# Norms, rotation and gates of two mixers placed beside the input projections, and another block order in the local attention

## The chip, the cores and the metric

The kernel runs on one core of one Trainium2 chip. The metric is the device time of one execution in microseconds (us), lower is better. The core has five engines with queues of their own: TensorE (PE in the rows; its weight loads PEld), VectorE (DVE), ScalarE (ACT), GpSimd (POOL) and SyncE (SP), which here issues the DMAs. They meet only at semaphores.

## The reference, cut to what matters

A block of four layers runs over 512 latent tokens and 256 context tokens of width 1024, all in float32. Layer 1 ("even") joins local attention with a gated linear recurrence; layer 2 is a retention layer; layers 3 and 4 join a convolution, a differential attention and a delta-rule recurrence. The change touches layer 1 and layers 3 and 4. Of layer 1:

```python
k_ctx = kv_heads(pc['a_k'], qk_g[1])                 # RMS norm per head of 64
q_lat = apply_rope(attn_q_heads(p['a_q'], qk_g[0]), cos, sin)
k_lat = apply_rope(kv_heads(p['a_k'], qk_g[1]), cos, sin)
a_lat = window_attention(q_lat, k_lat, kv_heads(p['a_v']), k_ctx, v_ctx, sink)
f = lb + (1.0 - lb) * sigmoid(f_raw)                 # gates of the recurrence
q_l = silu(b_q);  y = rms_norm(o) * silu(b_g)
def apply_rope(x, cos, sin):
    x1, x2 = xf[..., :half], xf[..., half:]
    return concatenate([x1 * cos - x2 * sin, x2 * cos + x1 * sin])
```

A block of 128 queries sees the 256 context keys and, if it lies in the latent part, the key blocks beside it. Blocks 0 and 1 are the context's own queries, so they see 2 key blocks; blocks 2 to 5 see 4, 5, 5 and 4. Of layers 3 and 4 the change touches how 24 rows of the projection become the gates of the delta rule: beta = sigmoid(b) and g = -exp(A_log) * softplus(a + dt_bias), summed along each chunk of 128 tokens, and exponentials of these sums.

## The kernel before, in words

Activations lie transposed: 128 channels down the partitions, the 768 tokens (context, then latent) along a row. A tile `core.u(t)` is such a strip. A projection (`Dense`, L267) makes output in groups of 256 columns: for each of 8 input tiles k, 2 halves f and each token segment it does three float32r matmuls of split high and low halves (L476 to L478). Two sets of banks alternate between groups, so group g+2 waits for group g to be evacuated. ScalarE evacuates a group, then makes the high half of the weights of group g+2 (L259), and VectorE the low half (L264). A `side` object hangs other work on this loop: `side.scalar` and `side.vector` are called after each group on these engines, `side.tensor` on TensorE after input tile 3 of a group, and `side.load` on SP between weight loads. In layer 1's projection (13 groups, 0 to 12) the side work is `Modulation` (L953): VectorE multiplies and adds conditioning weights (L1013, L1016), and TensorE sums them over partitions with one-column matmuls (L1035) in groups 1, 3, 5, 7 and 9.

Stages are blocks of instructions; at the end of each, all engines meet. After layer 1's projection come:

- `head_norm` "qk" (L1484): squares on ScalarE, sums per head by matmuls of 10 rows (L1535), root, reciprocal on VectorE (L1554), spread back by matmuls (L1546), multiply (L1561), for the five tiles of queries and keys.
- `rope_stage` (L1573): six tables by DMA; the rotated half by a matmul with a permutation (L1591); values transposed (L1593); multiply and add on VectorE and GpSimd; keys copied to both head halves by matmuls (L1598, L1599). Beside it ScalarE applies sigmoid and silu to 16 tiles (L1622 to L1624).
- `window_stage` (L1634): 24 steps, for each of 4 pairs of heads the blocks 0 to 5. TensorE makes scores of step s+2, turns the probabilities of step s in chunks (L1722) and weighs the values of step s-1 (L1735). ScalarE does the exponentials (L1769) and copies the turned chunks (L1778); VectorE takes the maximum (L1796), normalises (L1813) and takes the outputs away (L1820).
- `gla_stage` (L1832), the recurrence, and its norm.

In layers 3 and 4 the projection of 13 groups has `Convolutions` (L2510) as side work. Then `delta_gates_stage` (L2744) makes the gates and turns keys and values (24 transposes, L2766), and `mixer_stage` (L2828) runs delta rule and attention in one interleaved order. It opens with value transposes (L3088), while SP loads a table `dist` and four lambda vectors (L2903, L2905) that GpSimd waits for before it casts the table (L3269) and makes the first slope (L3220); the first attention scores (L3045, L3052) need both.

## Time and profile before

| | |
|---|---|
| time, median of 3 runs | 4082.05 us (4080.58 to 4082.73) |
| the profiled execution's own time | 4088.78 us |
| span of its trace | 4087.0 us |
| mean granted TensorE clock | 0.947 of full |
| PE busy | 3805.1 us (93%) |
| DVE busy | 2240.8 us (55%) |
| ACT busy | 1530.3 us (37%) |
| POOL busy | 341.6 us (8%) |

Shares of busy time are means over some forty stages. What a stage costs is read from where it starts and ends, and what binds it from the waits inside it.

### The profile page before, as it was taken

Reading aid. Unit: us, or ns where it says so; the run is one execution under the profiler, and the core shown is the slowest. Engines: PE = TensorE matmul, PEld = TensorE weight load, DVE = VectorE, ACT = ScalarE, POOL = GpSimd, SP = SyncE. Lnnn points to the kernel's source line nnn. Section 1 sums busy time; section 2 is a strip of 40 time slices with the busy share of each in tenths; the row PEclk is TensorE's granted clock in tenths of the full one; section 3 lists DMA queues with packets and bytes.
Section 4 is the critical chain, followed back from the end, with each engine's and each line's share of the span. In section 5 each row is a group of like instructions: output and inputs, shape, how many; then the busy total and the mean of one; then the engine's idle time right before and its main releaser. Section 6 shows DMA issues by size and latency. Waiting matters only on the chain. (4 is left out here: it accounts for less than half of the span.)

```text
span 4087.0 us, 49821 instructions
## 1 busy us (share of the span) xinstructions
PE 3805.1 (93%) x20537; PEld 3114.3 (76%) x20537; DVE 2240.8 (55%) x3209; ACT 1530.3 (37%) x2348; POOL 341.6 (8%) x292
## 2 busy tenths in 40 slices
PE   7998789999999999999999979989998979988998
PEld 4884567888887888878877758757787757867886
DVE  5724765545465444572266756544477856544375
ACT  2114632111354322352254335433365335533264
POOL 0000220000000000000000045200000034400000
PEclk9997879999999999999999979979999979988999
DMA  5510012333212121123222100022222200012231
GB/s 199 176 42 10 6 42 81 126 124 129 69 61 75 64 66 60 62 76 100 92 96 91 58 12 1 1 83 78 94 96 83 68 12 1 1 63 76 88 103 62
DMA packets 254721, 288.91 MB, mean 71 GB/s; under 512 B 6756, under 2 KB 226939, under 8 KB 254517
## 3 DMA queue, kind: packets, MB, share of 16 engines
q1 hardware_dynamic: 252437, 281.84, 21.4%
q10 hardware_dynamic: 2080, 4.19, 0.3%
q8 instruction: 146, 2.39, 0.2%
q14 instruction: 58, 0.48, 0.0%
HBM read 283.92 MB, written 2.10 MB: 70 GB/s over the span
## 5 line engine op out<-in xcount | busy, mean ns | idle before, releaser
L476 PE MATMUL banks<-h_halves,w_halves 128*128 128x512 f32 (+1 forms) x3728 | 1391.9, 373 | 56.3 <-DVE h_halves L264 32.4
L477 PE MATMUL banks<-h_halves,w_halves 128*128 128x512 f32 (+1 forms) x3728 | 1387.2, 372 | 0.0
L478 PE MATMUL banks<-h_halves,w_halves 128*128 128x512 f32 (+1 forms) x3728 | 1380.4, 370 | 0.0
L476 PEld LDWEIGHTS banks<-h_halves,w_halves 128*128 128x128 f32 x3728 | 713.5, 191 | 196.4 <-issue 49.4
L478 PEld LDWEIGHTS banks<-h_halves,w_halves 128*128 128x128 f32 x3728 | 711.5, 191 | 122.3
L477 PEld LDWEIGHTS banks<-h_halves,w_halves 128*128 128x128 f32 x3728 | 713.5, 191 | 117.6 <-issue 0.5
L264 DVE TENSOR_TENSOR w_halves<-work,w_halves 128x2048 fp32r<-128x2048 f32 (+1 forms) x212 | 481.3, 2270 | 434.8 <-ACT w_halves L259 434.5
L259 ACT ACTIVATE w_halves<-work 128x2048 fp32r<-128x2048 f32 (+1 forms) x212 | 401.4, 1894 | 409.0 <-PE banks L478 388.6
L259 ACT ACTIVATE h_halves<-kept 128x512 fp32r<-128x512 f32 (+1 forms) x520 | 332.1, 666 | 301.4 <-PE banks L478 231.5
L264 DVE TENSOR_TENSOR h_halves<-kept,h_halves 128x512 fp32r<-128x512 f32 (+1 forms) x520 | 360.8, 736 | 133.0 <-ACT h_halves L259 132.3
L1016 DVE SCALAR_TENSOR_TENSOR kept<-kept 128x512 f32<-128x512 f32 x280 | 188.2, 744 | 7.2 <-DMA kept<-in_mod_w 7.2
L758 ACT ACTIVATE kept<-kept 128x512 f32<-128x512 f32 x64 | 37.5, 631 | 234.3 <-DVE kept L752 234.2
L2211 PE MATMUL banks<-h_halves,w_halves 128*128 128x512 f32 x320 | 120.5, 377 | 3.7 <-DVE h_halves L1181 3.7
L1207 POOL TENSOR_TENSOR h_halves<-kept,h_halves 128x768 fp32r<-128x768 f32 (+1 forms) x8 | 13.6, 1706 | 1304.4 <-ACT kept L1174 1304.4
L773 ACT ACTIVATE kept<-banks 128x512 f32<-128x512 f32 x66 | 30.0, 530 | 245.3 <-PE banks L478 245.3
L2212 PE MATMUL banks<-h_halves,w_halves 128*128 128x512 f32 x320 | 118.9, 372 | 0.0
L2213 PE MATMUL banks<-h_halves,w_halves 128*128 128x512 f32 x320 | 118.5, 370 | 0.0
L752 DVE SCALAR_TENSOR_TENSOR kept<-banks,kept 128x512 f32<-128x512 f32 x64 | 41.0, 685 | 139.4 <-PE banks L478 139.4
L3265 POOL TENSOR_TENSOR work<-work 128x512 f32<-128x512 f32 x84 | 108.8, 1300 | 70.5 <-PE banks L2938 52.6
L3397 DVE TENSOR_TENSOR work<-work,banks 128x512 f32<-128x512 f32 x84 | 62.5, 744 | 94.3 <-PE banks L2958 94.3
L2227 PE MATMUL banks<-w_halves,h_halves 128*128 128x256 f32 x384 | 108.7, 283 | 0.0
L2226 PE MATMUL banks<-w_halves,h_halves 128*128 128x256 f32 x384 | 108.7, 283 | 0.0
(388 smaller groups left out, 4973.7 us busy)
## 6 DMA issues: line engine op xcount, KB each, us to landing
work<-in_w_ff SPq DMA_DIRECT2D x64, 1024.0 KB, 5.3
work<-in_ffn_w_in SPq DMA_DIRECT2D x44, 1024.0 KB, 5.1
kept<-in_mod_w SPq DMA_DIRECT2D x40, 1024.0 KB, 5.1
work<-in_odd_w_in SPq DMA_DIRECT2D x24, 1024.0 KB, 5.4
work<-in_w_in SPq DMA_DIRECT2D x24, 1024.0 KB, 5.0
work<-in_ffn_w_out SPq DMA_DIRECT2D x16, 1024.0 KB, 5.2
work<-in_even_w_in SPq DMA_DIRECT2D x13, 1024.0 KB, 5.1
work<-in_odd_w_out SPq DMA_DIRECT2D x8, 1024.0 KB, 5.1
```

Source lines behind the costliest of these rows:

```text
L259: return core.nc.scalar.activation(dst, src, ACT.Copy)
L264: return core.nc.vector.tensor_tensor(dst, src, high.bitcast(F32), ALU.subtract)
L476: nc.tensor.matmul(o, low[:, k - a, fc], rh[:, tc], start=(k == 0), stop=False)
L477: nc.tensor.matmul(o, high[:, k - a, fc], rl[:, tc], start=False, stop=False)
L478: mm = nc.tensor.matmul(o, high[:, k - a, fc], rh[:, tc], start=False, stop=(k == K - 1))
L1016: ins = nc.vector.scalar_tensor_tensor(out=self.sum(q, n), in0=self.slot(m)[:, k], scalar=c, in1=self.sum(q, n), op0=ALU.mult, op1=ALU.add)
L2211: nc.tensor.matmul(o, low[:, c, fc], rh, start=(c == 0), stop=False)
L2212: nc.tensor.matmul(o, high[:, c, fc], rl, start=False, stop=False)
L2213: mm = nc.tensor.matmul(o, high[:, c, fc], rh, start=False, stop=(c == KD - 1))
L2226: nc.tensor.matmul(o, core.h(c)[:, tc], low[:, c, :], start=False, stop=False)
L2227: mm = nc.tensor.matmul(o, core.h(c)[:, tc], high[:, c, :], start=False, stop=(c == KD - 1))
L3265: nc.gpsimd.tensor_tensor(c4(pl.level[m % 3]), c4(pl.s[h % 2]), mat(pl.pairs[:, cc(lv)]), ALU.mult).then_inc(level_masked, 1)
```

## The change

Layer 1: `head_norm` "qk" and `rope_stage` are gone. A new side object `QueriesKeys`, which holds the old `Modulation`, does their work inside the projection: squares, head sums in groups 1 to 3, root and reciprocal after group 3, spreads in groups 6 to 8, norm and rotation on GpSimd, with the rotated half fetched by DMA from partition to partition and its sign put into the sine table; values turned in group 9. Sigmoid and silu are applied as ScalarE evacuates a group (`EvenCopy`), which now takes both segments; the context segments of the two halves share one bank. The local attention starts at once and takes the blocks in another order.

Layers 3 and 4: the gate arithmetic moves into `Convolutions` (groups 8 to 12). `delta_gates_stage` becomes `turn_stage`: 24 transposes, their copies split between VectorE and ScalarE, and the loads and cast that opened `mixer_stage`.

```diff
@@ class Dense
+                if side is not None:
+                    side.load_last(sp, low_done, units)
...
                             if side is not None and k == 3:
                                 side.tensor(pe, i * B + j)
+                            if side is not None and k == 6:
+                                side.tensor_late(pe, i * B + j)
+class EvenCopy(Finish):
+        def scalar(act, g, j, f, banks, half, free, done):
+            func = self.FUNC.get(g, ACT.Copy)
+            nc.scalar.activation(core.u(2 * g + f)[:, LAT], banks[0], func).then_inc(free, 1)
+            if f == 1:
+                o = core.sb(U0 + 2 * g * T, 2 * T).rearrange("p (f t) -> p f t", t=T)[:, :, 0:CTX]
+                nc.scalar.activation(o, core.ps[:, 4 + j % 2, :].rearrange("p (f t) -> p f t", t=CTX), func).then_inc(free, 2)
+class QueriesKeys:
+    SQUARES = {1: (0, 1), 2: (2, 3), 3: (4,)}
+    SPREADS, SPREADS_LATE = {6: 0, 7: 2, 8: 4}, {6: 1, 7: 3}
+    COPIES = {6: (0, 1), 7: (2, 3), 8: (4,)}
+    def load(self, sp, at):
+        self.mod.load(sp, at)
...
+        if at == 9:
+            sp.wait_ge(self.scaled, self.N)
+            sp.dma_start(self.cos, core.const("cosA")).then_inc(self.tables_in, 16)
+            sp.dma_start(self.sin, core.const("sinA")).then_inc(self.tables_in, 16)
+            self.swap(sp, 0)
+            self.swap(sp, 1)
+        if at == 10:
+            for m in range(2, self.N):
+                sp.wait_ge(self.roped, m - 1)
+                self.swap(sp, m)
+            sp.wait_ge(self.roped, self.N)
...
+    def scalar(self, act, at):
...
+        if at == 4:
+            act.wait_ge(self.square_used, self.N)
...
+        for m in self.COPIES.get(at, ()):
+            act.wait_ge(self.spread, m + 1)
+            if m:
+                act.wait_ge(self.scaled, m)
...
+        if at == 12:
+            act.wait_ge(self.roped, self.N)
+    def vector(self, dve, at):
+        if at == 4:
+            dve.wait_ge(self.rooted, 2)
+            self.nc.vector.reciprocal(self.std, self.std).then_inc(self.rstd_done, 1)
+        self.mod.vector(dve, at)
+    def gpsimd(self, pool):
+        for m, x in enumerate(self.tiles):
+            pool.wait_ge(self.copied, 2 * m + 2)
+            nc.gpsimd.tensor_tensor(x, x, self.back, ALU.mult).then_inc(self.scaled, 1)
+        pool.wait_ge(self.tables_in, 32)
+        for m, x in enumerate(self.tiles):
+            pool.wait_ge(self.swapped[m % 2], 64 * (m // 2 + 1))
+            nc.gpsimd.tensor_tensor(x[:, LAT], x[:, LAT], self.cos, ALU.mult).then_inc(self.turned, 1)
+            nc.gpsimd.tensor_tensor(o, o, self.sin, ALU.mult).then_inc(self.turned, 1)
+            pool.wait_ge(self.turned, 2 * m + 2)
+            nc.gpsimd.tensor_tensor(x[:, LAT], x[:, LAT], o, ALU.add).then_inc(self.roped, 1)
@@ window_stage
-    steps = [(p, i) for p in range(4) for i in range(6)]
+    steps = [(p, i) for p in range(4) for i in (2, 0, 3, 4, 1, 5)]
...
-            pe.wait_ge(masks_ready, 2)
@@ class Convolutions, tensor
+        if j == 10:
+            pe.wait_ge(self.centred, 2)
+            pe.wait_ge(self.gate_dve, 5)
+            for d in range(2):
+                nc.tensor.matmul(core.ps[:, 4, d * 24:(d + 1) * 24].rearrange("p (c n) -> p c n", n=6), pl.cum[d],
...
+        if j == 11:
+            pe.wait_ge(self.gate_act, 5)
@@ second_layer
-    delta_gates_stage(core, nc, a, l, pl)
+    turn_stage(core, nc, a, l, pl)
@@ mixer_stage
-            sp.dma_start(pl.dist, core.const("dist")).then_inc(loads_in, 16)
...
-            pe.wait_ge(dist_made, 1)
```

How the change moves instructions is shown at three places. First TensorE inside group 7 of layer 1's projection, after input tile 3; L1035 (L1040 in the changed kernel) are the one-column sums. Before:

```order
L476 MATMUL banks<-h_halves,w_halves 128x256
L477 MATMUL banks<-h_halves,w_halves 128x256
L478 MATMUL banks<-h_halves,w_halves 128x256
L1035 MATMUL banks<-kept 128x1 x16
L476 MATMUL banks<-h_halves,w_halves 128x512
```

and of the changed kernel (L1180 and L1181 are the spreads of a tile's inverse norm):

```order
L476 MATMUL banks<-h_halves,w_halves 128x256
L1040 MATMUL banks<-kept 128x1 x16
L1180 MATMUL banks<-kept 128x512
L1181 MATMUL banks<-kept 128x256
L472 MATMUL banks<-h_halves,w_halves 128x512
```

Two matmuls have been put behind the sums; ten such pairs are spread over groups 1 to 8.

Second ScalarE between the evacuation of group 5 and that of group 7. Before (L657 evacuates, L259 makes the high half of weights):

```order
L657 ACTIVATE kept<-banks 128x512 x2
L259 ACTIVATE w_halves<-work 128x2048
L657 ACTIVATE kept<-banks 128x512 x2
L259 ACTIVATE w_halves<-work 128x2048
L657 ACTIVATE kept<-banks 128x512 x2
```

In the changed kernel (L728 and L731 evacuate, L250 makes the high half, L1150 copies a spread out of its banks):

```order
L728 ACTIVATE kept<-banks 128x512 x2
L731 ACTIVATE kept<-banks 128x2x256
L250 ACTIVATE w_halves<-work 128x2048
L1150 ACTIVATE kept<-banks,kept 128x512
L1150 ACTIVATE kept<-banks,kept 128x256
L1150 ACTIVATE kept<-banks,kept 128x512
L1150 ACTIVATE kept<-banks,kept 128x256
L728 ACTIVATE kept<-banks 128x512 x2
```

The copies stand between a weight split and the next evacuation.

Third TensorE from the end of the third layer's projection into its mixer; the branches are stage ends. Before:

```order
L2761 MATMUL banks<-kept 128x24 x4
L2766 MATMUL banks<-kept 128x128 x24
L2772 MATMUL banks<-work 128x24 x2
L2774 MATMUL banks<-work,kept 128x48
L2749 UNCONDITIONAL_BRANCH
L2907 UNCONDITIONAL_BRANCH
L3088 MATMUL banks<-kept 128x128 x12
L2923 MATMUL banks<-kept,work 128x128 x4
L3045 MATMUL banks<-work 128x512 x2
L3052 MATMUL banks<-p_halves 128x512 x6
```

Of the changed kernel:

```order
L2944 UNCONDITIONAL_BRANCH
L2948 MATMUL banks<-kept 128x128 x24
L2936 UNCONDITIONAL_BRANCH
L3043 UNCONDITIONAL_BRANCH
L3224 MATMUL banks<-kept 128x128 x12
L3059 MATMUL banks<-kept,stream 128x128 x4
L3181 MATMUL banks<-work 128x512 x2
L3188 MATMUL banks<-p_halves 128x512 x6
```

The gate matmuls (L2761, L2772, L2774) have left the stage; they now stand in groups 8 and 10 of the projection.

## Rows read from the trace of the kernel before

**Rows 1.** Busy time by stretch, layer 1 after its projection; columns start:end, length, engines.
```profile
core 0: us, PE busy (x) PEld busy (x) DVE busy (x) ACT busy (x) POOL busy (x), PEclk, DMA share, GB/s
313.80:344.40 30.60, 24.84 (x48) 9.76 (x48) 11.53 (x15) 5.94 (x9) 0.00 (x0) 0.72 0.00 1
344.40:366.70 22.30, 12.29 (x24) 5.35 (x24) 8.07 (x10) 15.70 (x11) 6.32 (x5) 0.70 0.13 41
366.70:464.50 97.80, 85.70 (x721) 59.87 (x722) 67.06 (x192) 62.34 (x186) 0.74 (x2) 0.95 0.01 1
```
**Rows 2.** Timeline at stage ends; columns start, duration, instruction, idle before and releaser.
```profile
313.79 1.08 ACT L657 ACTIVATE kept<-banks 128x512 f32<-128x512 f32 x2 [15.71 <-PE banks L478]
315.16 3.83 ACT L1522 ACTIVATE work<-kept 128x768 f32<-128x768 f32 x5 [0.28 <-PEq L431]
366.89 1.28 ACT L1767 ACT_TABLE_LOAD   x1 [0.26 <-PEq L1579]
```
**Rows 3.** Busy time by stretch, groups 2, 3, 5 and 9 of layer 1's projection.
```profile
110.30:127.10 16.80, 16.80 (x97) 14.70 (x96) 13.70 (x21) 2.89 (x4) 0.00 (x0) 1.00 0.61 191
127.10:149.00 21.90, 21.90 (x129) 19.55 (x128) 13.19 (x20) 2.87 (x4) 0.00 (x0) 0.92 0.43 144
165.80:189.30 23.50, 23.50 (x129) 20.93 (x128) 13.20 (x20) 2.88 (x4) 0.00 (x0) 0.85 0.46 150
244.80:263.40 18.60, 18.60 (x113) 16.49 (x113) 3.05 (x4) 2.89 (x4) 0.00 (x0) 1.00 0.18 57
```
**Rows 4.** Timeline, TensorE, spreads in group 10 of the third layer's projection.
```profile
2322.37 2.84 PE L2698 MATMUL banks<-kept 12*128 12x512 f32 x6
```
**Rows 5.** Timeline, VectorE: side work in group 5, and the reciprocals of stage "qk".
```profile
176.29 0.88 DVE L1013 TENSOR_SCALAR kept<-kept 128x512 f32<-128x512 f32 x2 [5.30 <-PE banks L1035]
177.09 9.36 DVE L1016 SCALAR_TENSOR_TENSOR kept<-kept 128x512 f32<-128x512 f32 x14
...
325.12 4.95 DVE L1554 RECIPROCAL work<-work 10x512 f32<-10x512 f32 x2 [10.44 <-ACT work L1525]
```
**Rows 6.** Busy time by stretch, local attention, six steps of one pair of heads.
```profile
402.30:424.50 22.20, 20.48 (x183) 14.42 (x181) 16.76 (x50) 15.18 (x46) 0.00 (x0) 1.00 0.01 1
```
**Rows 7.** Timeline, local attention: its first matmul, and VectorE's longest wait in that stretch.
```profile
367.70 0.55 PE L1699 MATMUL banks<-work,kept 64*128 64x256 f32 x1 [2.74 <-POOL work L1758]
...
413.82 0.29 DVE L1820 COPY kept<-banks 128x128 f32<-128x128 f32 x1 [1.41 <-ACT work L1778]
```
**Rows 8.** Timeline, the third layer's gate stage: first instruction, transposes, sums.
```profile
2360.61 1.28 ACT L2814 ACT_TABLE_LOAD   x1 [9.55 <-PEq L431]
...
2360.97 4.50 PE L2766 MATMUL banks<-kept 128*128 128x128 f32 x24
2370.09 1.05 PE L2772 MATMUL banks<-work 128*128 128x24 f32 x4 [4.61 <-DVE work L2795]
2370.96 0.64 PE L2774 MATMUL banks<-work,kept 128*128 128x48 f32 x2
```
**Rows 9.** Timeline, opening of the third layer's mixer.
```profile
2374.86 2.80 PE L3088 MATMUL banks<-kept 128*128 128x128 f32 x12 [3.26 <-PEq L2749]
...
2376.68 0.43 SPq L2905 DMA_DIRECT2D work<-in_diff_lambda_k  x1
...
2379.50 1.28 DVE L3312 SCALAR_TENSOR_TENSOR p_halves<-kept,p_halves 128x512 fp32r<-128x512 f32 x2
...
2381.76 1.21 POOL L3269 CAST work<-kept 128x896 f16<-128x896 f32 x1 [551.28 <-DMA work<-in_diff_lambda_k]
...
2384.04 1.01 PE L3045 MATMUL banks<-work 128*128 128x512 f16 x2 [5.53 <-POOL work L3220]
2384.98 1.65 PE L3052 MATMUL banks<-p_halves 32*128 32x512 f32 x6
```
**Rows 10.** Busy time by stretch, groups 8 and 11 of the third layer's projection.
```profile
2293.50:2304.40 10.90, 10.90 (x49) 9.01 (x49) 10.27 (x15) 3.89 (x4) 0.00 (x0) 1.00 0.30 96
2331.00:2348.10 17.10, 17.10 (x59) 11.79 (x58) 10.45 (x9) 3.84 (x3) 0.00 (x0) 0.90 0.00 1
```

More of the change, by code:

```diff
@@ L537, in _ @@
                     group(G // B, j)
-            if before is not None:
-                block.gpsimd(before.gpsimd)
+            @block.gpsimd
+            def _(pool):
+                if before is not None:
+                    before.gpsimd(pool)
+                if side is not None:
+                    side.gpsimd(pool)
             def wait_tile(eng, i, n):
@@ L2516 @@
     SEMS = 22
+    LOADS = 16 * 5
     PAD = CONV_K // 2
@@ L2806, in _ @@
-            chain.wait()
-            nc.vector.tensor_tensor(pl.ekd, core.ps[:, 7, 48:96], pl.gsum, ALU.subtract).then_inc(sums, 1)
-            dve.wait_ge(chain_a, 2)
-            nc.vector.scalar_tensor_tensor(out=pl.nbge, in0=pl.beta, scalar=-1.0, in1=pl.eg, op0=ALU.mult, op1=ALU.mult)
+            for b in range(0, 6, 2):
+                dve.wait_ge(turned, b + 1)
+                nc.vector.tensor_copy(dst(b), bank(b))
         @block.scalar
         def _(act):
-            act.wait_ge(turned, 1)
@@ L2822, in _ @@
[L2822 to L2825 removed]
+            for b in range(1, 6, 2):
+                act.wait_ge(turned, b + 1)
+                nc.scalar.activation(dst(b), bank(b), ACT.Copy)
+        @block.gpsimd
+        def _(pool):
+            pool.wait_ge(loads_in, 16 * 6)
+            nc.gpsimd.tensor_copy(pl.dist16, pl.dist)
@@ L3498, in second_layer @@
     cat = (0, 1, 4, 5, 6, 19, 20, 21)
-    into.run(f"in2_{l}", before=before, side=Convolutions(core, nc, l))
     pl = DeltaPlan(core)
-    delta_gates_stage(core, nc, a, l, pl)
+    into.run(f"in2_{l}", before=before, side=Convolutions(core, nc, l, a, pl))
+    turn_stage(core, nc, a, l, pl)
     mixer_stage(core, nc, a, l, pl)
```

440 lines of the change are left out of this document (244 added, 196 removed).

## The prediction, made before the changed kernel was run

> **What bounds the kernel now.** I read the page first: TensorE is busy 93% of the span, so what counts is where it is not doing projection matmuls. The timeline gave the stage ends, the table of stretches each stage's length, and the timeline inside a stage who waits for whom. Between layer 1's projection and its local attention lie two stages of 30.6 and 22.3 us [rows 1] in which no engine is full: in "qk" TensorE is busy 24.8 us, VectorE 11.5; in the rotation ScalarE 15.7 of 22.3, TensorE 12.3. The granted clock there is 0.72 and 0.70, a mixture of 1.2 and 2.4 GHz. These are chains, each link waiting for the one before. The projection is the opposite: a group without side work lasts 16.80 us at clock 1.00 with TensorE busy all of it, while ScalarE works 2.89 us of it and VectorE 13.7 [rows 3]. So work on the slack engines is free there and each matmul costs its full length. The same holds for layers 3 and 4: a gate stage that is a chain of tiny instructions, from 2360.61 us [rows 8] to the mixer's start at 2374.86 [rows 9], behind a projection whose groups take 10.90 us [rows 10].
>
> The sum is made against the profiled execution, 4088.78 us, which is 6.7 us (0.16%) above the median of the runs, 4082.05; I take the difference over to the median.
>
> **The two stages removed.** From the first instruction of "qk" at 315.16 to the first of the local attention at 366.89 are 51.7 us [rows 2]. What takes their place at the projection's end: the last evacuation, two activations in 1.08 us [rows 2], becomes three of about 512 elements on ScalarE, +0.5. VectorE's copies beside it fall away but ran in parallel. Gain 51.2.
>
> **What layer 1's projection takes on.** TensorE gets 5 head sums and 5 spreads, each of a 512- and a 256-column float32 matmul. Three such matmuls of 512 columns took 2.84 us at the full clock [rows 4], 0.95 each; half that for 256; 1.42 a pair, 14.2 for ten. The six value transposes: 24 took 4.50 [rows 8], so 1.1. Nothing covers them: TensorE is full there. To this comes the clock. Groups with 8, 16, 16 one-column sums last 18.60, 21.90 and 23.50 [rows 3]. Eight cost 1.8 (18.60 - 16.80), so sixteen should cost 3.6, but cost 5.1 and 6.7, and exactly these two groups show a clock of 0.92 and 0.85: side work of this kind is followed by a stretch at 1.2 GHz, worth 1.5 or 3.1 us. The new pairs are longer matmuls; three of them left the clock at 1.00 as far as [rows 4] go, since they took no more than 0.95 each. I add 1.7 us for one more such stretch, most likely in group 7, where a pair stands right behind sixteen sums. The bounds are 0 and nine places times 3.1, 28. Total +17.0.
>
> The page of the Trainium skill on this, "TensorE: Matmul & The Clock Gate", section "What's actually happening", has the clock follow how busy TensorE has been. [Rows 3] do not agree as it stands: TensorE shows busy for 23.50 of 23.50 us in the group whose clock is 0.85. By the rule the new pairs would cost no clock and the sum below would be 1.7 us better; I go by the row.
>
> The other engines there cost nothing, and this is their cover. ScalarE: per group 0.5 for the context, squares of 0.8 each, copies of about 1 us, table loads of 1.28 [rows 2], at most 6 us more on 2.9 in a group of 16.8. Its copies in groups 6 to 8 wait for spreads after input tiles 3 and 6; behind them in its queue stands the next evacuation, which is due only at the group's end, one input tile (2.1 us) after the later spread, and TensorE needs its banks a whole group later. VectorE: the reciprocals, 4.95 us [rows 5], come after group 3 ahead of 10.2 us of conditioning work [rows 5]. VectorE then finishes some 4 us into group 5, and the sums in the middle of group 5 that wait for it are due 8.4 us in: hidden, with 4 us to spare. It loses its own evacuations, 0.75 a group. GpSimd does 5 multiplies and 15 rotation operations, 1.2 to 1.7 us each as in the stages before; with DMA hops of 3 to 5 us between tiles the rotation takes 25 to 35 us from the middle of group 8 and is due only before group 12's evacuation, some 60 us later. SP's queue: the load of unit 12 stands behind the wait for the norms in group 8 and is due two groups later. No cost; if any cover were gone, it would be a few us once.
>
> **The local attention.** Its first matmul waited for GpSimd's casts until 367.70 [rows 7], 0.8 us after the stage began; these casts are now earlier. It also begins right after full-clock matmuls instead of at 1.2 GHz, worth another 0.7 in its first steps. The block order: six steps take 22.20 us, TensorE busy 20.48, VectorE 16.76, ScalarE 15.18 [rows 6]. The waits are latencies of the loop maximum, exponentials, normalise, turn, copy; the longest of VectorE's four in this stretch is 1.41 us [rows 7]. Light blocks between heavy ones fill some of them, but the same five-block steps 3 and 4 still stand side by side, and the stage now starts with a heavier block. Following the queues with these durations I find each pair of heads about 0.5 us shorter, and as much lost again at the two ends. Bounds: better by 4 x (22.20 - 16.76) = 21.8, if only VectorE bound it; worse by two waits of 1.41 more per pair, 11.3. I take 0. Together -1.5.
>
> **The gate stages, twice.** Before, 14.25 us (2360.61 to 2374.86) [rows 8, 9]. After: the transposes, 4.9 us with the first copies behind them, run beside six DMAs. The last lambda vector is issued 1.8 us into the stage and landed 5.1 after its issue (2376.68 to 2381.76 [rows 9]), that is at 6.9; the larger table behind it in the same queue may add 1; then the cast, 1.21 [rows 9], and the stage end, 0.3: 9.4. Gain 4.9. What is late there is now GpSimd's load, no longer the chain.
>
> Then the mixer's opening. TensorE waited until 2384.04 for GpSimd's slope, itself behind the cast [rows 9]: the three-pass scores L3052 start at 10.12 us into the stage. With loads and cast gone the next to be late is VectorE's split, 2379.50 + 1.28 [rows 9], 5.92 us in. So they start at 6.0, 4.1 earlier, and the chain behind them moves along: GpSimd's own opening work, 5 us, no longer binds. Per layer 9.0, twice 18.0. Bounds per layer: 4.1 alone if the loads land as late as the old stage ended, and 11 if they land after 4 us.
>
> **What the second projection takes on.** Four small transposes and three small matmuls, ten instructions; six of them took 1.05 + 0.64 [rows 8], the rest about 0.9: 2.6 per layer, full price, in groups 8 and 10. The side work of group 11 made it 17.10 us where 10.90 is the rule, at clock 0.90 [rows 10], so a low-clock stretch of 1.5 more can follow in group 10; I keep that for the range. TensorE's new wait in group 11 for ScalarE's exponentials comes 5.4 us into the group by the queue's durations, where TensorE arrives at 5.45: a tie. Behind it are group 11's sums and spreads. Twice 2.6 is +5.2.
>
> **Sum:** -51.2 + 17.0 - 1.5 - 18.0 + 5.2 = -48.5. From 4082.05: 4033.5 us (profiled: about 4040).
>
> **Rivals.**
> 1. The clock. Each of the nine new places in layer 1's projection is followed by a low-clock stretch like group 5's. For it: [rows 3], three groups of one-column sums out of five show it. Against: [rows 4] do not. Price 28 - 1.7, so 4060.
> 2. The order pays. The waits of [rows 7] vanish halfway between TensorE's limit, 4 x (22.20 - 20.48) = 6.9, and VectorE's 21.8: 14 better, 4019.5. Against: the chain through one step is unchanged.
> 3. Slower than before. ScalarE waits before group 12's evacuation for the end of the rotation (a chain SP, DMA, GpSimd, SP through five tiles). From the middle of group 8 it has some 60 us until it delays anything, and must lose 48 more before the gain is gone: it would have to take 108 us, over 20 a tile, where its three operations and one hop come to 7. Then 4085 and more, us for us. Nothing in the rows supports it but that no such hop was measured.
> 4. The loads do not gain in the gate stages: DMAs of broadcast vectors, now with a table behind them, land later and the stages shorten by 2 instead of 4.9. Then 4039.
>
> **Chances:** forecast with its small deviations 0.66, clock 0.10, order 0.10, loads 0.12, slower 0.02. The predicted time is 4033.5. The range 4020 to 4048 holds the forecast, the loads, half of the order's case and the milder half of the clock's. A measurement of this kernel tells 0.2%, about 8 us, from no change; only rival 3 comes near, so faster 0.97, same 0.01, slower 0.02.
>
> **What would show it.** In the changed profile: layer 1's groups 1 to 3 and 6 to 9 longer by 1.4 to 3 us each and none by more than 4.5; the attention's first matmul within 2.5 us of the projection's last; no wait of TensorE on GpSimd's rotation; the attention 94 to 98 us; turn stages of 9 to 10 us ended by GpSimd's cast; the mixer's first scores about 6 us in. The forecast is wrong if the projection's clock falls below 0.9 over its length, or if a stage after it changes in length, which I take to be none.

## The result, and the profile after

The changed kernel takes 4047.55 us, median of 3 runs (4046.64 to 4048.96), against 4082.05: ratio 0.9917, 95% interval 0.9894 to 0.9939, 34.5 us faster. Run again on another chip it took 4042.13 (ratio 0.9896, 0.9881 to 0.9912). The forecast was 4033.5. The direction was right, and 14 of the 48.5 us are missing. From trace to trace the kernel lost 39.8 us (spans 4087.0 and 4047.2), 8.7 less than forecast. The other 5.3 come from the base: the profiled execution of before lay 6.7 us above its median, that of the changed kernel 1.4 above its own.

The profiled execution took 4048.96 us, its span is 4047.2. The time between the first instructions of the stages shows where the gain lies. "Again" is the second trace of the same kernel. Brackets in the column of before give the range over all four traces with that code (before, e2, e3, e4).

| us | before | after | after again | forecast of the difference |
|---|---|---|---|---|
| start of the local attention | 366.9 | 331.3 | 331.2 | -34.2 |
| local attention | 97.5 | 100.6 | 100.9 | -1.5 |
| recurrence | 102.9 | 105.6 | 105.4 | 0 |
| eight stages, to the third layer's projection | 1625.7 | 1625.8 | 1625.7 | 0 |
| projection and gate or turn stage, layer 3 | 181.9 | 180.5 | 180.0 | -2.3 |
| mixer, layer 3 | 296.8 (292.6 to 296.8) | 294.1 | 290.0 | -4.1 |
| projection and gate or turn stage, layer 4 | 196.0 | 194.0 | 192.3 | -2.3 |
| mixer, layer 4 | 296.7 (293.3 to 296.7) | 292.8 | 288.9 | -4.1 |

The busy time by stretch of the changed kernel answers to [rows 3]: groups 3, 5, 6, 7 and 8 of layer 1's projection, then group 12, the attention's first 3.9 us, the attention, and the recurrence.

```profile
core 0: us, PE busy (x) PEld busy (x) DVE busy (x) ACT busy (x) POOL busy (x), PEclk, DMA share, GB/s
132.10:155.60 23.50, 23.50 (x133) 19.88 (x132) 12.45 (x17) 5.38 (x6) 0.00 (x0) 0.93 0.39 123
172.40:194.30 21.90, 21.90 (x129) 19.53 (x128) 16.24 (x23) 4.66 (x5) 0.00 (x0) 0.92 0.60 195
194.30:214.50 20.20, 20.20 (x105) 16.16 (x105) 12.36 (x17) 5.50 (x9) 7.68 (x2) 1.00 0.60 205
214.50:241.20 26.70, 26.70 (x137) 21.72 (x136) 12.45 (x17) 5.46 (x8) 7.46 (x3) 0.87 0.13 41
241.20:259.70 18.50, 18.50 (x102) 15.46 (x101) 2.29 (x1) 4.43 (x6) 3.25 (x3) 1.00 0.35 107
...
312.60:329.40 16.80, 16.72 (x96) 14.47 (x94) 0.00 (x0) 1.53 (x3) 0.00 (x0) 1.00 0.00 0
...
331.10:335.00 3.90, 3.71 (x14) 2.40 (x14) 0.78 (x1) 1.28 (x1) 0.00 (x0) 0.56 0.00 0
...
331.10:431.90 100.80, 86.23 (x721) 60.70 (x721) 67.71 (x192) 61.73 (x186) 0.00 (x0) 0.94 0.00 1
431.90:537.50 105.60, 86.33 (x920) 76.86 (x920) 86.02 (x142) 51.43 (x67) 39.85 (x24) 0.76 0.02 6
```

The groups bear out the working: group 3 takes one pair on (21.90 to 23.50), group 6 two (16.8 to 20.2) at full clock, group 7 two beside its sums, with more low clock than before (21.9 to 26.8 at 0.87), group 8 one (16.8 to 18.5). Group 5, which takes nothing on, lost 1.6 us of low clock (23.50 to 21.90), but where such stretches fall varies: e2 has before's projection, and its groups 3, 5 and 7 last 23.5, 21.9 and 23.5 us for before's 21.9, 23.5 and 21.9. The attention's row is the one to stop at: 100.80 us with the same 721 matmuls that took 97.80 [rows 1]. The recurrence behind it has the same 920 matmuls too and is 2.7 us longer than before:

```profile
464.50:567.40 102.90, 83.50 (x920) 74.31 (x920) 85.62 (x142) 51.39 (x67) 39.87 (x24) 0.78 0.02 7
```

The timeline of the changed kernel, at the attention's start and at its end. Columns as in [rows 2].

```profile
331.26 1.28 ACT L1881 ACT_TABLE_LOAD   x1 [0.27 <-PEq L424]
335.87 0.20 ACT L1881 ACTIVATE kept<-kept 128x2 f32<-128x2 f32 x1 [3.33 <-DVE kept L1916]
335.99 0.67 ACT L1883 ACTIVATE work<-banks,kept 128x512 f32<-128x512 f32 x1
...
428.82 0.29 DVE L1934 COPY kept<-banks 128x128 f32<-128x128 f32 x1 [2.36 <-ACT work L1892]
429.26 1.97 PE L1855 MATMUL banks<-work,kept 128*64 128x128 f32 x16 [0.64 <-DVE kept L1934]
431.27 0.29 DVE L1934 COPY kept<-banks 128x128 f32<-128x128 f32 x1 [2.16 <-PE banks L1855]
431.84 1.28 ACT L1992 ACT_TABLE_LOAD   x1 [2.81 <-PEq L1806]
431.88 5.36 PE L2173 MATMUL banks<-kept 128*128 128x128 f32 x24 [0.65 <-PEq L1806]
```

The first exponential comes 4.7 us into the stage (335.99 against 331.26). Before it came 3.1 in, since block 0 has two key blocks and block 2 four (with the old order in the changed kernel it comes 2.5 in, e1, or 2.0, e12):

```profile
366.89 1.28 ACT L1767 ACT_TABLE_LOAD   x1 [0.26 <-PEq L1579]
...
369.96 0.46 ACT L1769 ACTIVATE work<-banks,kept 128x256 f32<-128x256 f32 x1
```

At the other end the last lines tell more. The last 16 weighing matmuls take 1.97 us, and the recurrence's first 24 transposes take 5.36 us, where the same instruction took 2.81 before. The rows show a granted clock of 0.50 there, TensorE's lower level. The stretches of the changed kernel's last steps:

```profile
424.00:428.00 4.00, 2.34 (x19) 1.64 (x18) 1.41 (x5) 0.88 (x2) 0.00 (x0) 0.88 0.00 0
428.00:432.00 4.00, 2.71 (x20) 1.97 (x20) 0.58 (x2) 0.97 (x3) 0.00 (x0) 0.50 0.00 0
432.00:436.00 4.00, 4.00 (x20) 4.00 (x21) 3.17 (x5) 1.13 (x1) 0.00 (x0) 0.50 0.48 131
```

Layer 3 after its projection, answering to [rows 8, 9]:

```profile
2333.74 2.81 PE L2948 MATMUL banks<-kept 128*128 128x128 f32 x24 [1.65 <-PEq L424]
...
2336.11 0.43 SPq L2942 DMA_DIRECT2D work<-tables  x1
...
2336.59 0.60 ACT L2962 ACTIVATE work<-banks 128x512 f32<-128x512 f32 x1 [0.27 <-PE banks L2948]
2342.55 0.93 POOL L2967 CAST work<-kept 128x896 f16<-128x896 f32 x1 [541.78 <-DMA work<-tables]
2343.81 2.79 PE L3224 MATMUL banks<-kept 128*128 128x128 f32 x12 [7.26 <-PEq L2936]
...
2349.97 1.65 PE L3188 MATMUL banks<-p_halves 32*128 32x512 f32 x6 [0.35 <-DVE p_halves L3445]
```

The turn stage lasts 10.1 us, and all its work is done by 2337.2, 3.5 us in. What ends it is GpSimd's cast, which waits for the sixth load, issued at 2336.11, until 2342.55. The mixer's three-pass scores start 6.16 us into it, as forecast (6.0), released by VectorE's split.

### The profile page after: what moved, and what is told of

It reads as the page before. It is cut to its first block and busy times, and to the rows that moved or that the text cites. A ratio compares the mean times of both kernels' runs of the same rounds, so it can differ in the third digit from the quotient of the medians.

```text
span 4047.2 us, 49776 instructions
## 1 busy us (share of the span) xinstructions
PE 3786.3 (94%) x20511; PEld 3106.7 (77%) x20511; DVE 2215.3 (55%) x3156; ACT 1541.4 (38%) x2377; POOL 375.5 (9%) x307
## 5 line engine op out<-in xcount | busy, mean ns | idle before, releaser
L250 ACT ACTIVATE w_halves<-work 128x2048 fp32r<-128x2048 f32 (+1 forms) x212 | 401.5, 1894 | 403.2 <-PE banks L476 382.9
L250 ACT ACTIVATE h_halves<-kept 128x512 fp32r<-128x512 f32 (+1 forms) x520 | 332.0, 665 | 302.0 <-PE banks L476 232.6
```

The source lines that it names most:

```text
L250: return core.nc.scalar.activation(dst, src, ACT.Copy)
```

## The experiments

Times are medians. Each ratio is to runs of before on the same chip; the experiments ran on four chips, where before took 4080.1 to 4084.0. The old order in the changed kernel comes first, since the attention's row asks for it.

**e1, the block order undone in the changed kernel; e12, the same again.**

```diff
-    steps = [(p, i) for p in range(4) for i in (2, 0, 3, 4, 1, 5)]
+    steps = [(p, i) for p in range(4) for i in (0, 1, 2, 3, 4, 5)]
```

> The changed kernel with the blocks of the local attention back in the order 0 to 5, all else kept. In the changed kernel this stage lasts 100.6 us where it lasted 97.5, against 96 forecast, and the recurrence behind it 105.6 where it lasted 102.9 with no edit. Theory A (the order costs): its first step now has a heavy block (first output 1.6 us later in the stage), each pair of heads takes 22.45 instead of 22.20, and the tail 0.5 more. Then this kernel's attention stage is 97 to 98 us, and the kernel is 2.5 to 3.5 us faster than the changed one, 38 faster than before (4044). Theory B (the order is neutral; the stage is longer because of where it starts, right behind full-clock matmuls, and what clock it is granted): the stage stays at 100 to 101 and the time at 4047 to 4048. On the recurrence: if its 2.7 us come from the order they go too (another -2.7, 4041); if they are the luck of where a low-clock stretch falls, they stay or move without a pattern.

Measured: 4035.40 us (4028.74 to 4046.43), ratio 0.9885 (0.9867 to 0.9903). Attention 97.0, recurrence 102.4. The stage is as theory A says, and the recurrence shortens too. The median is 12.2 us below the changed kernel's, but the two intervals overlap (the changed kernel's is 0.9894 to 0.9939), so what the order costs is read from the stages, over more traces.

**e11, the changed kernel again, beside e12.**

> The changed kernel once more, on the same chip as the next one, to measure what the block order is worth in pairs: from the traces 7.0 us (attention 3.55, recurrence 3.2), from the medians of two calls 12. Its time 4047 to 4048. If the recurrence shows 105.6 again with transposes of 5.4 us, that cost belongs to the order; if it shows 102.4 or 99.8, it is luck.

> The changed kernel with the blocks in the order 0 to 5, a second time, beside the run above. Its time was 4035.4 over a wide range (4028.7 to 4046.4). If the order costs 7 us by stages and the rest is scatter, this gives 4038 to 4041; if 12 is real, 4035. Its recurrence is 99.8 or 102.4, never 105.6, if the 2.8 us at the stage's boundary are the order's.

Measured: e11 4042.13 (ratio 0.9896, 0.9881 to 0.9912), e12 4034.60 (0.9885, 0.9871 to 0.9899). By stages: attention 100.9 against 95.9, recurrence 105.4 against 102.4. Over seven traces with the old order behind the new projection (e1, e12, e6, e15, e7, e10, e13) the attention takes 95.5 to 97.0, mean 96.4, and the recurrence 99.8 to 102.8, mean 101.9. The new order in after and after again takes 100.7 and 105.5: 4.3 + 3.6 = 7.9 us. The two pairs of medians give 12.2 and 7.5, with intervals that overlap. The transposes at the boundary take 5.26 in e11 and 2.81 in e12.

The attention's share belongs to the order. The recurrence's share comes with it three times out of four: e3 keeps the new order and shows 101.1, 105.5 and transposes of 5.36, but e9, which starts the stage 17.8 us later with the same order, shows 99.5, 103.1 and 2.81. Its last steps are as sparse and keep their clock (L1937 and L2176 are L1934 and L2173 of the changed kernel):

```profile
440.60:444.60 4.00, 2.34 (x27) 1.68 (x27) 1.51 (x6) 1.26 (x4) 0.00 (x0) 1.00 0.00 0
444.60:448.60 4.00, 2.53 (x31) 1.83 (x30) 0.58 (x2) 1.26 (x4) 0.00 (x0) 1.00 0.00 0
```
```profile
428.13 0.29 DVE L1937 COPY kept<-banks 128x128 f32<-128x128 f32 x1 [0.44 <-ACT work L1895]
448.02 0.29 DVE L1937 COPY kept<-banks 128x128 f32<-128x128 f32 x1 [1.28 <-PE banks L1858]
448.63 2.81 PE L2176 MATMUL banks<-kept 128*128 128x128 f32 x24 [0.65 <-PEq L1809]
```

The two copies are the last of the third pair of heads and the last of the fourth, 19.9 us apart. In the changed kernel they are 21.2 apart:

```profile
410.04 0.29 DVE L1934 COPY kept<-banks 128x128 f32<-128x128 f32 x1 [0.44 <-ACT work L1892]
...
431.27 0.29 DVE L1934 COPY kept<-banks 128x128 f32<-128x128 f32 x1 [2.16 <-PE banks L1855]
```

**e2, the new order alone, in the kernel before.** The same line edited in before, with its count of scored steps made independent of the order.

> The kernel before with the new block order alone. Theory A: the attention stage grows from 97.5 by 2.5 to 3.5 us, the time from 4082 to about 4085 (ratio 1.0007). Theory B: the stage keeps its 97.5 and the time its 4082. A forecast by the working made before the run was 0 with bounds of -21.8 and +11.3.

Measured: 4087.64, ratio 1.0009 (1.0000 to 1.0018). The attention grew from 97.5 to 100.4, as theory A says. The recurrence stayed at 102.9: the stage's tail is as sparse here, but it ran at full clock, and the transposes took 2.81 (columns: stretch, length, PE busy, PEclk, DMA share, GB/s).

```profile
459.00:463.00 4.00, 2.34 (x30) 1.00 0.00 0
463.00:467.00 4.00, 2.50 (x31) 1.00 0.00 0
```

So 3 us come with the order anywhere. The fall of the clock in the tail, with what it costs there and behind the stage, needs more than the order: it is there in after, e11 and e3 and not in e2 and e9. What decides whether a sparse tail loses its clock these rows don't say.

**e5, the last pair of heads in the old order; e14, only the first pair in the new one.**

```diff
+ e5:  for i in ((2, 0, 3, 4, 1, 5) if p < 3 else (0, 1, 2, 3, 4, 5))
+ e14: for i in ((2, 0, 3, 4, 1, 5) if p < 1 else (0, 1, 2, 3, 4, 5))
```

> The changed kernel, where only the last pair of heads takes its blocks in the order 0 to 5; the three pairs before keep 2, 0, 3, 4, 1, 5. In the changed kernel TensorE is busy 2.3 to 2.7 of each 4 us over the last steps, the granted clock falls to 0.50 before the stage ends, and the next stage's first 24 transposes take 5.36 us instead of 2.81. Theory A (what the order costs behind the stage comes from its last steps: a light block just before the last): with the last pair in the old order the transposes take 2.8 again and the recurrence 102.4, while the attention keeps the cost of its first step and of three pairs, 99 to 100 us; in all 3 to 4 us faster than the changed kernel's profiled 4049. Theory B (the clock falls there because of where the whole stage stands): the transposes stay at 5.4.

> The changed kernel with the new block order in the first pair of heads alone. The order costs 3.6 to 4 us in the attention; with the last pair undone 1.6 of them are left (98.2 against 96.6, the mean of four runs of the old order). If these are the first step (four key blocks instead of two before the first exponential), this kernel's attention is 97.7 to 98.2; if they are a steady 0.25 in each pair, it is 96.9. The recurrence stays at 99.8 to 102.8 by either, and its first transposes at 2.8.

Measured: e5 4045.96 (0.9918, 0.9905 to 0.9932), e14 4036.12 (0.9896, 0.9880 to 0.9912). The transposes took 2.81 in both, and e5's tail ran at full clock:

```profile
425.00:429.00 4.00, 3.15 (x43) 2.60 (x44) 0.51 (x2) 1.26 (x3) 0.00 (x0) 1.00 0.00 0
429.90:433.90 4.00, 2.81 (x24) 2.60 (x24) 3.65 (x5) 2.39 (x2) 0.00 (x0) 1.00 0.46 131
```

The attention took 98.2 in e5 and 98.4 in e14, the recurrence 99.8 and 101.4. Where the order's cost lies is seen from VectorE's last copy of each pair of heads, in us:

| run | order of the pairs | stage's start to first pair | second | third | fourth |
|---|---|---|---|---|---|
| before, e4 | old | 32.3 | 22.2 | 22.2 | 20.3 |
| e2 | new | 35.0 | 22.45 | 22.45 | 19.9 |
| seven traces behind the new projection | old | 30.3 to 31.8 (mean 31.2) | 22.2 | 22.2 | 20.3 |
| e14 | new in the first | 33.2 | 22.2 | 22.2 | 20.3 |
| e5 | new in the first three | 33.1 | 22.45 | 21.8 | 20.3 |
| after, e11 | new | 33.9, 34.0 | 22.45 | 22.45 | 21.2, 21.4 |
| e9 | new | 34.2 | 22.45 | 22.45 | 19.9 |

So the 4.3 us of the stage are 2.8 in the first pair, 0.25 in each of the next two and 1.0 in the last. The light block last but one does not cost that 1.0 by itself: where the clock holds (e2, e9) the last pair is 0.4 us shorter than in the old order. The fall to half clock costs 1.4 in the stage, and 2.5 in the next stage's transposes. The first pair varies by 1.5 us between executions of the old order, so its 2.8 is good to about 1 us; e2 against before gives 2.7.

By the medians e5 gains nothing clear over the changed kernel (0.9918 beside 0.9917 and 0.9896), where its attention and recurrence are 8.1 us shorter. This is left open: the intervals are 0.13% wide to either side, and the mixers alone move by more than 5 us from execution to execution.

**e8, another order.**

```diff
+    steps = [(p, i) for p in range(4) for i in (0, 2, 3, 1, 4, 5)]
```

> The changed kernel with the block order 0, 2, 3, 1, 4, 5: starts light, keeps the two five-block steps apart, ends in two heavy ones. If the cost of 2, 0, 3, 4, 1, 5 was its heavy first step and its light last but one, this order has neither: attention 96 to 98 us, recurrence 102.4, like the order 0 to 5 (4035). If parting the heavy blocks shortens a pair below 22.20 it is 1 to 2 us better than that; the forecast's bounds for a pair are 16.8 and 25.0.

Measured: 4039.68, ratio 0.9904 (0.9889 to 0.9919); attention 97.2, recurrence 99.8. A light start and a heavy end give back the stage's loss: the first pair takes 31.4 us and the last 20.3. Parting the two five-block steps does not shorten a pair: the two in the middle take 22.45 us each, as in the new order, against 22.2.

**e4, the kernel before again.**

> The kernel before once more, unchanged, for how much its stages vary between executions. Its profiled execution lay 6.7 us above the median of its other runs, and five unedited stages differ by -2.1 to +2.7 us between the two traces. If the trace's stages repeat within 0.3 us, such differences are effects of the change; if unedited stages move by 1 to 3 us here too, they are the clock's luck, and the sum of 8.7 us missing between the traces is not all to be explained by edits. Ratio 1.000 expected.

Measured: 4082.61, ratio 0.9999. Every stage repeats within 0.2 us but one, layer 4's mixer: 293.3 us where the first trace had 296.7. So the differences in unedited stages between before and after are not luck of one execution: the recurrence's +2.7 and the -2.1 to +1.4 of the stages behind it stand in e11 as well. Those behind the recurrence cancel to 0.1 us (the table's fourth line).

**e3, layers 3 and 4 undone.** The side work, the gate stage and the mixer's opening as before, layer 1 as changed.

```diff
-    into.run(f"in2_{l}", before=before, side=Convolutions(core, nc, l, a, pl))
-    turn_stage(core, nc, a, l, pl)
+    into.run(f"in2_{l}", before=before, side=Convolutions(core, nc, l))
+    delta_gates_stage(core, nc, a, l, pl)
```

> The changed kernel with the gate stages, the projection's side work and the opening of the mixer of layers 3 and 4 as they were before; layer 1 stays changed. By the terms of the forecast this takes 18.0 back and 5.2 away: 12.8 us slower than the changed kernel, 4060.4. By the stages of the two traces (gate stages 3.9 and 4.6 shorter, mixers 2.75 and 3.9 shorter, projections 2.5 longer each) it is 10.1 slower: 4057.6. Rival: the mixers' own length varies by some us from run to run for reasons of the clock, and then the worth of the part lies anywhere from 4 (the gate stages less the projections) to 13.

Measured: 4056.75, ratio 0.9936 (0.9923 to 0.9950). That is 9.2 slower than the changed kernel's first median and 14.6 than its second. Its mixers took 292.6 and 296.0 with the old opening, so a mixer's length says little from one trace. The intervals of e3 and of the changed kernel overlap (0.9923 to 0.9950, 0.9894 to 0.9939), those of e3 and e11 do not.

**e7, the loads back at the mixer's opening; e6 and e15, the loads issued in the turn stage and waited for in the mixer.** Both on e1.

```diff
  e6, in the turn stage (no cast there, nothing waits):
+            sp.dma_start(pl.dist, core.const("dist")).then_inc(core.table_in, 16)
  e6, in the mixer, GpSimd:
+            pool.wait_ge(core.table_in, 16 * (l + 1))
+            nc.gpsimd.tensor_copy(pl.dist16, pl.dist).then_inc(dist_made, 1)
             slope(0)
```

> The kernel with the old block order, all six loads and the cast back at the opening of the mixer of layers 3 and 4; only the gate arithmetic stays in the projection. The turn stage is then 3.8 us, and the mixer's first three-pass scores come 10.1 to 10.6 us into it: together 14.0 to 14.4 where the changed kernel has 10.07 + 6.16 = 16.2. By this the moved loads gained nothing and cost 2 us a layer: 4 us faster than the old-order kernel, 4031. By the forecast's working the moved loads were worth 4.1 in the opening and the stage was 4.9 shorter; it did not ask what the stage would be without them.

> The kernel with the old block order, and the turn stages of layers 3 and 4 no longer ended by GpSimd's cast: the loads are still issued at the stage's start, but on semaphores of their own, the cast waits in the mixer for its table alone, and the lambdas and the pair table are waited for where they are used. Theory: the turn stage of 10.1 us has work for 3.5 and then waits for the last landing 8.8 us in, so it shrinks to 3.8, while the mixer's first three-pass scores stay at about 6 us, bound by VectorE's split: 6.2 us a layer, 12.5 in all less what low-clock stretches give or take (1.6 to 3.4 us a mixer), 4024 against 4035.4. Rival: the table lands no sooner than the lambdas, then the cast ends 11 us after the turn stage's start and the scores at 12.5, a gain of 3.7 a layer. Rival 2: the mixer takes the time back entirely, as it took back 1.4 in layer 3; then 4035.

> The kernel with the old order and the early loads again (4026.7, ratio 0.9867), on the same chip as the one with the sums in halves, so that the two can be compared in pairs. Expected 4024 to 4029; its mixers anywhere from 288 to 293.

Measured: e7 4036.28 (0.9888), e6 4026.70 (0.9867, 0.9851 to 0.9882), e15 4023.76 (0.9867). In all three the turn stage is 3.7 us. In e7 the three-pass scores start 11.05 us into the mixer, 14.8 in all where the changed kernel has 16.2, but its mixers then took 297.6 twice, and the time is e1's and not the 4031 expected. In e6 they start 5.56 in, 9.3 in all:

```profile
2331.53 0.93 POOL L3401 CAST work<-kept 128x896 f16<-128x896 f32 x1 [538.93 <-DMA kept<-tables]
2331.56 1.50 PE L3220 MATMUL banks<-kept 128*128 128x128 f32 x12 [0.93 <-PEq L2937]
...
2337.10 0.96 PE L3184 MATMUL banks<-p_halves 32*128 32x512 f32 x6 [1.45 <-DVE p_halves L3445]
```

GpSimd casts at once: the table, issued at 2327.91, had landed by the stage's end, within 3.6 us. What was late in the changed kernel was the tail of six loads, for which a cast waited that needs the first alone. Moving the loads was worth about nothing by itself. Splitting the wait made each turn stage 6 us shorter and was worth 7 us by the ratios (0.9867 for 0.9885, intervals that overlap) and 8 to 11 by the medians, less than the 12.5 that the theory counted.

**e9, each spread of layer 1's projection issued twice.**

```diff
-        nc.tensor.matmul(core.ps[:, 6, :], pick, self.std[:, LAT], start=True, stop=True)
+        for _ in range(2):
+            nc.tensor.matmul(core.ps[:, 6, :], pick, self.std[:, LAT], start=True, stop=True)
+        nc.tensor.matmul(core.ps[:, 7, 0:CTX], pick, self.std[:, 0:CTX], ...)
```

> The changed kernel with each of the five spreads of layer 1's projection issued twice (the second overwrites the first): ten more float32 matmuls in groups 6 (2 pairs), 7 (2) and 8 (1), nothing else. By the price of the forecast, 1.42 us a pair, the three groups grow by 2.84, 2.84 and 1.42 from the changed kernel's 20.16, 26.77 and 18.47, in all 7.1 us. Rival (each further place is followed by a stretch at 1.2 GHz worth 1.5 to 3.1 us): 8 to 16 us more on top, group 6 above 26. In the changed kernel group 6 took 3.36 for two pairs, group 7 4.86 with 16 one-column sums beside them, which would say that only group 7's clock (0.87) pays.

Measured: 4058.41, ratio 0.9935 (0.9923 to 0.9947). The attention starts 17.8 us later. Groups 6, 7 and 8 of e9:

```profile
194.70:221.40 26.70, 26.70 (x113) 20.60 (x113) 12.36 (x17) 5.52 (x9) 7.07 (x2) 0.84 0.47 156
221.40:255.50 34.10, 34.10 (x145) 26.42 (x145) 12.45 (x17) 5.47 (x9) 4.76 (x2) 0.75 0.10 32
255.50:277.50 22.00, 22.00 (x105) 17.92 (x105) 2.29 (x1) 4.39 (x6) 4.02 (x3) 0.89 0.32 95
```

They grew by 6.5, 7.3 and 3.6 where the matmuls account for 3.4, 3.4 and 1.7 (two spread pairs took 3.35 us, 213.83 to 217.18). The rest is clock: two spread pairs at one place are followed by a stretch at 1.2 GHz, one is not. Two pairs of head sums at one place are not either: they took 2.74 us (107.33 to 110.07 in the changed kernel), and groups 1 and 2, which hold them, ran at 1.00 in every trace:

```profile
112.40:132.10 19.70, 19.70 (x105) 15.42 (x105) 12.36 (x17) 4.85 (x7) 0.00 (x0) 1.00 0.60 199
```

The rival that the forecast gave a chance of 0.10 is true of places twice as large. With the places as they are it did not come.

**e10, one spread moved out of group 7; e13, also the sums in halves.** On e6.

```diff
  e10
-    SPREADS, SPREADS_LATE = {6: 0, 7: 2, 8: 4}, {6: 1, 7: 3}
+    SPREADS, SPREADS_LATE = {6: 0, 7: 2, 8: 3}, {6: 1, 8: 4}
  e13, in tensor (after tile 3) and in tensor_late (after tile 6)
-        self.mod.tensor(pe, j)
+        self.mod.tensor(pe, j, slice(0, 1))
...
+        self.mod.tensor(pe, j, slice(1, None))
```

> The kernel with the old block order and the early loads (4026.7 us), and in layer 1's projection the second spread of group 7, which has the 16 one-column sums, moved to group 8. If a group with sums and two pairs is what brings the long low-clock stretch (26.77 us at 0.87 where 21.9 + 2.84 = 24.7 were due), group 7 falls by 1.42 + 2.0 to 23.3 and group 8 grows by 1.42 to 19.9: 2 us faster, 4024.7. If the stretch comes with the sums alone, only the pair moves and the time stays.

> The kernel with the old block order, the early loads and the moved spread, in which the 16 one-column sums of groups 3, 5 and 7 are issued as 8 after input tile 3 and 8 after tile 6; nothing is added or left out but one wait of TensorE for a copy. Theory: a piece of float32 side work of 2.8 us and more is followed by about 7 us at 1.2 GHz (3.5 us lost), a piece of 1.8 is not (group 9 with 8 sums keeps 1.00; two spreads at one place in group 6 took it from 1.00 to 0.84). Then group 5 falls from 21.9 to 20.4, group 3 from 23.5 to 21.8, group 7 from 25.2 to 21.8 (its first piece has 8 sums and a spread, 3.2 us, and may still bring a stretch, then 25): 3 to 6.5 us faster than the 4028 of the kernel it is built on. Rival: the clock follows the amount of side work in a group and not its pieces; then the groups keep their lengths and the time.

Measured: e10 4028.31 (0.9865, 0.9850 to 0.9880), e6's time. Group 7 fell to 25.1 and group 8 rose to 20.2: the pair moved, the stretch stayed with the sums. e13 4019.53 (4016.34 to 4020.74), ratio 0.9853 (0.9838 to 0.9868). Its groups 3, 5, 6 and 7:

```profile
132.80:154.70 21.90, 21.90 (x134) 18.68 (x133) 12.46 (x17) 5.44 (x8) 0.00 (x0) 1.00 0.34 105
171.50:191.80 20.30, 20.30 (x129) 18.23 (x128) 15.69 (x23) 4.59 (x6) 0.00 (x0) 1.00 0.60 205
191.80:212.00 20.20, 20.20 (x106) 16.16 (x105) 12.36 (x17) 5.54 (x10) 8.19 (x2) 1.00 0.64 208
212.00:235.50 23.50, 23.50 (x134) 20.30 (x133) 14.03 (x17) 4.43 (x8) 2.17 (x2) 0.93 0.14 45
```

The sums of group 5 in e13, and in the changed kernel:

```profile
179.16 1.84 PE L1041 MATMUL banks<-kept 128*128 128x1 f32 x16
```
```profile
180.60 3.63 PE L1040 MATMUL banks<-kept 128*128 128x1 f32 x32
```

Group 3 has the same 16 sums and its pair at clock 1.00 in 21.90, group 5 its 16 sums in 20.30; the 32 records of the changed kernel are its 16 sums, two to each. These are the lengths that instructions alone give (16.8 + 3.6 + 1.42 and 16.8 + 3.6). Group 7, whose first piece is 8 sums and a pair, still shows 0.93.

Groups 3 and 5 by themselves don't prove it. The same sums in one piece kept 1.00 in group 3 of e6, e7 and e11 and in group 5 of e5 and e12. Group 3 of e11, and group 5 of e12:

```profile
132.10:154.10 22.00, 22.00 (x135) 18.66 (x134) 12.45 (x17) 5.39 (x6) 0.00 (x0) 1.00 0.40 133
```
```profile
172.50:192.90 20.40, 20.40 (x131) 18.30 (x130) 16.32 (x24) 4.66 (x5) 0.00 (x0) 1.00 0.64 208
```

But no trace with one piece kept 1.00 in both groups, and in e5, e6 and e12, where one group did, group 7 took 28.4 us for 26.8. Taken together the projection, from the end of group 0 to that of group 12, lasts 233.7 us in e13 and 236.9 to 238.5 in the twelve other traces that have the same matmuls. So the evidence that the piece counts, and not the amount in a group, is 3 to 5 us in one trace. The medians point the same way, 4.2 us below e15 on the same chip, with intervals that overlap (0.9838 to 0.9868, 0.9850 to 0.9883). e13 is the fastest kernel of this study, 4019.5 us, by three edits together (old order, split wait, sums in halves): 28 us below the changed kernel's first median and 60.6 below before on the same chip.

## Why the forecast was right or wrong

**Stages removed and the projection: right.** -51.2 and +17.0 gave -34.2; the attention starts 35.6 us earlier. Within the projection, from the end of group 0 to that of group 12, 222.1 us became 238.5, +16.4. That the sum is this near is in part luck. Head-sum pairs took 1.4 to 1.6 for 1.42, but spread pairs 1.7 (3.36 for the two of group 6), 1.3 more for the five. The stretch came in group 7 (+1.5), but group 5 lost 1.6, so low clock added nothing where 1.7 stood, and the transposes took 0.65 for 1.1. Group 7 grew by 4.8, beyond the 4.5 that the forecast allowed.

**The local attention: this step failed.** It read: "Light blocks between heavy ones fill some of them ... I find each pair of heads about 0.5 us shorter, and as much lost again at the two ends ... I take 0." The stage took 100.6 us where the forecast allowed 94 to 98. The runs put in place of the 0 for the order +4.3 us in the stage. The pairs in the middle are 0.25 us longer and not 0.5 shorter. The start costs 2.8, since the heavy block delays the first exponential (4.7 us into the stage for 2.0 to 2.5). The last pair is 0.4 shorter when the clock holds, but over steps that leave TensorE 2.3 us of work in 4 it fell to 0.50 in the changed kernel, +1.4. Then +3.6 in the recurrence, of which 2.5 are its first 24 transposes at half clock; that this follows from the order at the place where the stage stands is shown (after, e11, e3 against seven traces), why it does not in e2 and e9 is open. The forecast listed the upper bound (+11.3) and then gave a chance to the order's gain alone, none to its loss. In the traces, which miss 8.7 us of the forecast, the attention misses 4.6 (+3.1 for -1.5), the recurrence 2.7 and layers 3 and 4 another 2.7, while the attention's start is 1.4 better. The other 5.3 us between the medians are the base: a sum read from an execution 6.7 us above its median was set on the median. With the order undone the kernel takes 4035, 1.5 above the forecast; that it comes so near is in part luck, since layers 3 and 4 fall short there too while the attention's start and the recurrence (101.9 for 102.9) do better.

**The 0.7 us for a start "right after full-clock matmuls": not found in the changed kernel.** Group 12 runs at 1.00, and the attention's first 3.9 us at 0.56, after 2 us in which TensorE had nothing to do; before's first 3.9 us show 0.64. With the old order the stage takes 96.4 us for before's 97.5, so 1.1 of the 1.5 came. The Trainium skill has a page on such falls, "TensorE: Matmul & The Clock Gate", section "HAM oscillation — how this bites in real kernels": there long waits between bursts of matmuls throw the clock back. The rows agree with it in part. The changed kernel's tail falls to 0.50 over rows with TensorE busy 2.34 and 2.71 of 4 us; e2's and e9's tails, busy 2.34 and about 2.5, do not; and group 7 lost its clock while busy 26.70 of 26.70 us, which idle time cannot explain.

**"A stage after it changes in length, which I take to be none": wrong.** The recurrence grew by 2.7. Behind it unedited stages moved by -2.1 to +1.4 us and happened to cancel.

**Gate stages and mixer openings: right in kind, but 18.0 was 15.0.** The turn stages ended as the forecast said, by GpSimd's cast, at 10.1 and 9.5 us for 9.4; in layer 3 the sixth load, issued 2.4 us in, had landed 6.4 later, at 8.8 and not at 7.9. That is 4.1 and 4.9 less than before, for 4.9 each. The opening gained 3.96 of 4.1. The gain then lasts through most of the mixer: VectorE's 19th maximum is 231.0 us into it before and 226.4 after. Behind it a low-clock stretch takes 1.4 back, seen from that maximum to the next, first before, then after:

```profile
2605.80:2616.20 10.40, 8.77 (x67) 6.76 (x66) 5.70 (x15) 4.94 (x12) 3.69 (x4) 1.00 0.01 2
```
```profile
2570.10:2581.80 11.70, 10.07 (x65) 8.07 (x66) 5.66 (x15) 4.95 (x12) 3.69 (x4) 0.85 0.01 1
```

Sixteen mixers with the changed opening last 288.8 to 295.1 (mean 292.3), eight with the old one 292.6 to 296.8 (mean 295.3): 3.0 each. What varies lies at the mixer's end: in the eight mixers of layer 3 with the changed opening the 24th and last maximum comes 276.2 to 276.6 us in, and the whole mixer lasts 290.0 us (three) or 294.1 to 294.3 (five). So 4.1 + 4.9 + 2 x 3.0 = 15.0. Less what the projections take on, 5.6, layers 3 and 4 are worth 9.4 us by stages and 9 to 15 by medians (e3 against after and e11); the forecast had 18.0 - 5.2 = 12.8. What the forecast did not ask is whether the moved loads should end a stage at all (e6).

**The second projection: right.** +5.2 forecast, 2.8 and 2.9 found (in layer 4 of e11 and e12 only 1.0): from TensorE's first instruction in it to the first of the stage behind it 167.75 us became 170.56 in layer 3.

**Rivals.** The clock (0.10): not as the kernel stands, but e9 shows how near it was. The order pays (0.10): the reverse. No rival had the order cost anything. Slower by the rotation chain (0.02): it ends at 288.1, 41 us before ScalarE asks for it at 329.4. Loads without gain (0.12): no, the stages shortened by 4.1 and 4.9 and not by 2.

## What to carry to other kernels

An edit whose bounds reach to both sides needs a chance on both sides; an order of steps is judged first at its two ends (what stands before the first result, and how busy the full engine is over the last steps), since there nothing covers a wait and the next stage can inherit a lowered clock. A sum read from one trace is best compared with a trace: its execution may stand some us off the median. Work that TensorE does beside its main stream is worth trying in small pieces spread over the stream. A load should be waited for by the instruction that reads it, not by a stage end.

## What the runs showed of the hardware

- A matmul stream in which the profile shows no pause can still lose its clock. With 16 one-column sums in one piece (3.6 us), 43 of 48 groups show 0.75 to 0.93 and five show 1.00; with two pieces of 1.84 us groups 3 and 5 show 1.00 (e13, one trace). Two spread pairs in one piece (3.35 us) bring 0.84 in group 6 (e9), two pairs at two places 1.00, two pairs of head sums in one piece of 2.74 us 1.00. A group pays about 1.5 or 3.1 us for it, group 7 as much as 4.6 (28.4 us in e5, e6 and e12).
- Whether a sparse tail loses its clock can't be told from its busy time: 2.34 of 4 us went with a fall to 0.50 in three traces and with 1.00 in two (e2, e9). Where it fell, the next stage's 24 transposes took 5.26 to 5.36 us for 2.81.
- Most stages repeat within 0.2 us between executions of one kernel, others jump. The recurrence took 99.8 to 103.1 us, or 105.4 to 105.6 behind a tail at half clock; the mixers took anything from 288 to 298; one kernel's two traces (after, after again) differ by 13.8 us of span, all but 0.6 of it behind the third layer's turn stage.
- Of six loads issued in a row, the first had landed within 3.6 us of its issue (e6); the sixth, issued 2.3 us after the first, took 6.4 (changed kernel).
